# Router scores and squares of a hybrid decoder layer, made for two output blocks at a time in four column groups

## The reference, cut to what matters

```python
x = x + mix                                   # mix = m @ w_out
h = rmsnorm(x, ffn_norm_w)                    # x * rsqrt(mean(x*x) + 1e-6) * w
logits = h @ w_router + b_router              # 1024 -> 32 scores for each token
top_v, top_i = lax.top_k(logits, 4)
gate = softmax(top_v)
x = x + moe(h, top_i, gate)                   # 32 experts, gate_up 1024x2048, down 1024x1024
```

## Time and profile before

| what | value |
|---|---|
| median of 3 runs | 1414.34 us (1414.23 to 1415.02) |
| profiled execution, its own time | 1416.62 us |
| its span, first to last instruction | 1414.3 us |
| mean granted clock of TensorE | 0.995 |
| TensorE busy | 1376.6 us, 97% |
| VectorE, ScalarE, GpSimd busy | 36%, 18%, 8% |
| DMA over the span | 340 GB/s mean, about 430 GB/s in the experts |

### The profile page before, as it was taken

How to read it: one execution, slowest core, us unless ns; L and a number is a source line. 1 busy time by engine, 2 the same in 40 slices (tenths; PEclk the granted TensorE clock), 3 DMA queues, 4 the chain that set the end, 5 groups by cost and what they waited for, 6 DMA issues and landing times.

```text
span 1414.3 us, 17959 instructions
## 1 busy us (share of the span) xinstructions
PE 1376.6 (97%) x7571; PEld 669.2 (47%) x7571; DVE 511.7 (36%) x1090; ACT 255.6 (18%) x467; POOL 108.6 (8%) x107
## 2 busy tenths in 40 slices
PE   8999999999999999999999999999999999999996
PEld 6888885578887533333333333333323333333332
DVE  5655344313112219322432342223422234223423
ACT  3443341122200221111101110111111011011102
POOL 0102110100000001000100010001000011000100
PEclk9999999999999999999999999999999999999999
DMA  7532527554639799999999999999999999999995
GB/s 232 209 129 85 180 76 236 188 176 145 228 120 373 300 413 428 427 428 431 432 428 427 429 432 430 430 427 430 430 429 430 427 430 434 424 428 427 427 427 228
DMA packets 81807, 481.16 MB, mean 340 GB/s; under 512 B 13919, under 2 KB 34831, under 8 KB 61587
## 3 DMA queue, kind: packets, MB, share of 16 engines
q1 hardware_dynamic: 80644, 478.58, 83.1%
q10 hardware_dynamic: 986, 1.08, 0.3%
q0 software_dynamic: 96, 0.33, 0.1%
HBM read 468.85 MB, written 11.26 MB: 339 GB/s over the span
## 4 chain that ended last, share of the span: by engine, by line
PE 81%; DMA 16%; DVE 2%; issue 0%; ACT 0%; DVEq 0%; ACTq 0%
PE bank L1280 25%; PE bank L1304 12%; DMA ring<-in_w_gate_up 11%; PE bank L724 7%; PE bank L712 6%; DMA ring<-in_w_down 5%; PE bank L1252 5%; PE bank L1123 4%; PE bank L993 4%; PE bank L1334 3%; PE bank L1146 2%; DVE Ssg L2204 1%; PE bank L697 1%; PE bank L1260 1%; PE bank L1289 1%; PE bank L1344 1%
## 5 line engine op out<-in xcount | busy, mean ns | idle before, releaser
L1280 PE MATMUL bank<-ring,xT 128*64 128x512 f32 x2048 | 475.5, 602 | 12.1 <-DMA ring<-in_w_gate_up 11.1
L1280 PEld LDWEIGHTS bank<-ring,xT 128*64 128x64 f32 x2048 | 135.7, 137 | 282.5 <-issue 259.0
L2418 DVE TENSOR_TENSOR glu<-bank,bgb 128x512 f32<-128x512 f32 x32 | 22.1, 691 | 569.5 <-PE bank L1280 555.2
L1304 PE MATMUL bank<-ring,acT 128*64 128x512 f32 x992 | 218.7, 592 | 0.9 <-DMA ring<-in_w_down 0.8
L1304 PEld LDWEIGHTS bank<-ring,acT 128*64 128x64 f32 x992 | 71.1, 137 | 142.1 <-issue 140.8
L724 PE MATMUL bank<-HT,wslot 128*128 128x264 f32 x512 | 119.5, 389 | 0.0
L1918 POOL PARTITION_BROADCAST bgb<-hrow x31 | 40.8, 1317 | 979.5 <-DVE lin L2419 768.3
L724 PEld LDWEIGHTS bank<-HT,wslot 128*128 128x128 f32 x512 | 95.3, 190 | 19.7 <-issue 4.6
L712 PE MATMUL bank<-HT,wslot 128*128 128x264 f32 x384 | 89.5, 394 | 0.8 <-DVE HT L1965 0.8
L1252 PE MATMUL bank<-hrow,O 128*64 128x512 f32 x372 | 89.6, 599 | 0.0
L712 PEld LDWEIGHTS bank<-HT,wslot 128*128 128x128 f32 x384 | 73.9, 194 | 15.3 <-issue 2.3
(11 more groups left out here) (429 smaller groups left out, 1167.2 us busy)
## 6 DMA issues: line engine op xcount, KB each, us to landing
ring<-in_w_gate_up SPq DMA_DIRECT2D x44, 4096.0 KB, 26.7
ring<-in_w_down SPq DMA_DIRECT2D x62, 2048.0 KB, 25.3
ring<-in_w_gate_up SPq DMA_DIRECT2D x36, 2048.0 KB, 28.4
wslot<-in_w_in SPq DMA_DIRECT2D x17, 2048.0 KB, 8.2
ring<-in_w_gate_up SPq DMA_DIRECT2D x8, 1024.0 KB, 8.9
out<-Ssg SPq DMA_DIRECT2D x8, 512.0 KB, 5.3
Ssr<-in_state_ret SPq DMA_DIRECT2D x4, 1024.0 KB, 10.3
out<-Ssr SPq DMA_DIRECT2D x4, 1024.0 KB, 8.5
```

Of the source, the lines that this page charges most:

```text
L1280: t = pe.matmul(B[part][64 * g:64 * g + 64, :], block_of(xT, k), w[:, D * part + 512 * g:D * part + 512 * g + 512], start=(k == 0), stop=( ...
L1304: t = pe.matmul(home[64 * g:64 * g + 64, :], block_of(acts, 2 * k + a), w[:, D * a + 512 * g:D * a + 512 * g + 512], start=(k == 0 and a = ...
```

## The change

Scores and squares of two blocks are taken together, each in its own group of 32 columns, so that the two halves of each sum lie apart (scores in partitions 0 to 31 and 32 to 63, squares in 64 to 95 and 96 to 127). `scores(n)` stands in blocks 2, 4 and 6 and once after the blocks. The copy `lgc` has 128 partitions. The turn to tokens becomes two matmuls for each tile of tokens instead of one transpose: lgc's lower half by a constant whose column j is 1 in every row that is j modulo 32 (`C_D4`), which adds the two halves of the scores into bank 1, and its upper half by one column of that constant, which adds the squares into a column of bank 2.

```diff
-        lgc = at("lgc", ct0, [64, TOK])
+        lgc = at("lgc", ct0, [P, TOK])
@@ out_block
-                    if m and k == 4:
-                        score(m - 1)
+                    if m % 2 == 0 and m and k == 4:
+                        scores(m // 2 - 1)
@@
-            def score(m):
-                if m == 0:
-                    pe.wait_ge(s_wr, 32)
-                pe.wait_ge(s_xw, m + 1)
-                pe.matmul(B[2][0:32, 0:TOK], wr[:, m, :], XwT[:, m, :], start=(m == 0), stop=(m == KT - 1))
-                pe.wait_ge(s_sqt, m + 1)
-                pe.matmul(B[2][32:64, 0:TOK], K[:, C_ONE:C_ONE + 32], sqt[:, m % 2, :], start=(m == 0),
-                          stop=(m == KT - 1)).then_inc(s_lg, 1)
+            def scores(n):
+                if n == 0:
+                    pe.wait_ge(s_wr, 32)
+                pe.wait_ge(s_xw, 2 * n + 2)
+                pe.wait_ge(s_sqt, 2 * n + 2)
+                for g in range(4):
+                    m = 2 * n + g % 2
+                    lhsT, rhs = (wr[:, m, :], XwT[:, m, :]) if g < 2 else (K[:, C_ONE:C_ONE + 32], sqt[:, m % 2, :])
+                    t = pe.matmul(B[2][32 * g:32 * g + 32, 0:TOK], lhsT, rhs, start=(n == 0), stop=(n == KT // 2 - 1))
+                t.then_inc(s_lg, 1)
@@ after the blocks
-            score(KT - 1)
+            scores(KT // 2 - 1)
             normed_rows(4)
             pe.wait_ge(s_lgc, 1)
             pe.wait_ge(s_ob, 8)
             for c, r in TILES:
-                t = pe.transpose(B[1][0:r, 64 * c:64 * c + 64], lgc[:, P * c:P * c + r], K[0:64, C_ID:C_ID + 64])
+                pe.matmul(B[1][0:r, 64 * c:64 * c + NE], lgc[0:64, P * c:P * c + r], K[0:64, C_D4:C_D4 + NE],
+                          start=True, stop=True)
+                t = pe.matmul(B[2][0:r, c:c + 1], lgc[64:P, P * c:P * c + r], K[64:P, C_D4:C_D4 + 1], start=True, stop=True)
             t.then_inc(s_lt, 1)
@@ ScalarE
-                after(act, s_lg, 1, m - 1)
+                after(act, s_lg, 1, m // 2)
                 nc.scalar.activation(sqt[:, m % 2, :], XT[:, m, :], ACT.Square).then_inc(s_sqt, 1)
-            act.wait_ge(s_lg, KT)
-            nc.scalar.copy(lgc[:, :], B[2][0:64, 0:TOK]).then_inc(s_lgc, 1)
+            act.wait_ge(s_lg, KT // 2)
+            nc.scalar.copy(lgc[:, :], B[2][:, 0:TOK]).then_inc(s_lgc, 1)
@@
-                sums = B[1][0:r, 0:192].rearrange("p (c n) -> p c n", c=3)[:, first:last, 32:33]
-                nc.scalar.activation(rs[0:r, first:last].unsqueeze(2), sums, ACT.Sqrt, bias=eps[0:r, :], scale=1.0 / D
+                nc.scalar.activation(rs[0:r, first:last], B[2][0:r, first:last], ACT.Sqrt, bias=eps[0:r, :], scale=1.0 / D
```

## The result

The changed kernel takes 1410.84 us (median of 18 runs, 1408.88 to 1412.43) against 1413.85 us of the kernel before beside it (18 runs, 1411.25 to 1415.02): a ratio of 0.9981, with a 95% interval of 0.9975 to 0.9987, or 2.7 us by the ratio. The forecast was 1411.7 us, a gain of 2.7 us. The two medians themselves lie 3.0 us apart.

The account below looks back on a forecast made before the run. The prediction took TensorE's chain to the first expert as the bound, DMA stream following. Blocks 3.03, last visit −0.02 and turn −0.35 gave 2.66 us: 1414.34 − 2.7 = 1411.7 us, range 1409.7 to 1412.9.

Parts of the forecast that it names:

- The bound: Up to the first expert, TensorE's chain sets the time; shifts there reach the end one to one, DMA stream included.
- A visit and its groups: Breaking off output blocks for scores and squares: 0.77 us with two groups, 0.78 with four; blocks gain 3.03 us.
- the slot longer by 0.07 us: Alternative for four-group visits in the blocks: each slot 0.07 us longer, 0.4 us in all over three visits.
- a visit in pairs: Rival in the output blocks: four groups run two by two, 1.26 us a visit, total gain 0.75 us; chance 0.05.
- the change of shape: Within a score in the output blocks: about 0.28 us lost changing from 128 columns to 32 and back.
- New waits: In the output blocks: no visit waits for squares; block 4's weights land with 2.4 us to spare, costing nothing.
- The last visit: After the last block: all four passes start with the squares; loss 0.02 us, at most 0.07.
- The turn: Turn to tokens: six matmuls take 0.74 us against 0.39 for three transposes, a loss of 0.35 us.
- The sum: Whole path to the first expert: 3.03 − 0.02 − 0.35 = 2.66 us gained.
- The clock: Around the gather, 480.9 to 487.8 us: the low clock costs up to 3.4 us and may become cheaper or dearer.
- one sign of being wrong from my own list: Around the gather: forecast wrong if the stretch at 0.5 of the clock changes in length or place.
- a cheaper clock: Rival around the gather: low clock falls elsewhere or not at all, up to 3.4 us more won; chance 0.20.

Follow-up runs that it names:

- before_warm: Kernel before with three more float32 matmuls, outputs unused, in the waits between turn and gather: 1413.97 us, ratio 1.000.
- pairs: Kernel before with two blocks scored per visit, one after the other in the two old column groups, turn unchanged: 1412.33 us, ratio 0.9983.
- second comparison: The changed kernel, unaltered, measured once more beside the kernel before: 1409.96 us against 1413.93, ratio 0.9972.
- turn_alone: Kernel before with only the turn changed, six matmuls in place of three transposes: 1414.07 us, ratio 1.0002.
- late: Changed kernel with blocks 0 to 5 scored in one visit in block 7, eight buffers for squares: 1410.93 us, ratio 0.9983 to the kernel before.

## Why the prediction was right, and where it was off

**The bound.** It was to be the chain over TensorE to the first expert, with the DMA stream moving along. The profiles show it. The path from the first block to the gather was made anything from 36.23 to 41.75 us long, and from the gather to the end it stayed at 931.8 to 932.5 us in eight profiles, at 933.0 in that of `before_warm`, and at 935.1 only in the one with the low clock (932.1 without its 3.07 us). Behind the first expert the chain does go over loads of the ring (DMA has 16% of it on both pages), but these are sent as TensorE releases a block, and so they moved along. TensorE's waits for weights in the experts went from 11.1 us to 13.1 us in the first profile of the changed kernel and to 10.6 in the second, without changing that. But its reason, that the DMA engines stand empty then, held only in part: they ran full to 481.3 us, past the start of the first expert.

**A visit and its groups.** Forecast 0.77 us before and 0.78 us after; measured 0.77 and 0.79. Four groups ran in the slots of two, 0.22 us each, so the slot longer by 0.07 us that the prediction estimated as an alternative did not come; a visit in pairs, for which 1.26 us were forecast, cost 1.22 in `pairs`. The blocks lost 3.01 us, forecast 3.03 (its 5.37 is seven times the unrounded 0.767). The split within a visit was off by little: 0.28 us was put down to the change of shape and is 0.34.

**New waits.** None came. Between visits 32 passes run in 7.32 us, 0.2 us over 32 × 0.2227, and with the 0.58 us booked to the visit that is its 0.78 again; block 4 did not wait for its weights.

**The last visit.** Forecast +0.02 us and at most 0.07; measured +0.09 in the chain. All four matmuls now wait for ScalarE's squares of block 7 ("0.20 <-ACT sqt" in the row of 470.14 us), where the first pair waited for VectorE's scaled rows. So the visit starts 1.05 us after the blocks where it was 0.91, and gets 0.05 back by being shorter. It is the step furthest off in proportion, by 0.07 us.

**The turn.** Forecast 0.74 us, a loss of 0.35; measured 0.74 us in the chain, where the old one was 0.34: a loss of 0.40, and the turn alone shows the same 0.40. The missing 0.05 us is one of reading: the forecast set the new turn against 0.39 us, from the first start to the last end in the timeline, and the chain counts 0.34 for it. The row groups paired, and the tile of 8 tokens did begin 0.20 us after the pass before it instead of 0.11.

**The sum.** 3.01 − 0.09 − 0.40 − 0.04 = 2.48 us on the path against 2.66; the interval of the measured 2.7 us (1.8 to 3.5 us) holds both. That 2.7 comes so near to 2.66 is luck: the second comparison gave 4.0 us. The level, 1410.84 us for 1411.7, was met less well; 0.5 of the 0.9 us is that the kernel before lay at 1413.85 and not at 1414.34. The gain is below the 2.8 us that I had put as what can be told from no change, but the interval of its ratio leaves 1 out.

**The clock.** Here one sign of being wrong from my own list came: the stretch at 0.5 of the clock is not in the profile of the changed kernel. So the first expert came at 480.90 us and not at 482.8; and the DMA engines ahead of it were not at 13 GB/s but at 407. I gave a cheaper clock 0.20, and the profile looks like that rival; but all nine later profiles are without the stretch too, two of kernels with all seven visits in the blocks among them. So its absence doesn't tell what the change did. What the runs show is that it cost 3.07 us in one profile of the kernel before, and that 11 of 74 timed runs of that kernel lay at 1416 us and more. No run of the changed kernel in 26 went over 1412.5 us, but two of the 12 of `turn_alone` did reach 1417.5 and 1419.1 us (clocks of 0.993 and 0.995), and one of the 12 of `late` 1415.4 (0.995), 4.5 us over its median. So the case may be rarer or cheaper after the change; that stays open. It doesn't carry the 2.7 us of the first comparison, where no run of the kernel before lay over 1415.02.

## What to carry to other kernels

Where a small matmul of another shape is wedged into a dense stream, count the visits before the work in them: here a visit cost 0.34 us and a set of two or four column groups 0.45 us. Fill the groups, put sets in a row, and look for a place on the path where the engine waits anyhow; a dearer turn at the end (0.40 us) is paid once. And when a change is worth less than the scatter of the launch, compare lengths of stages within one profile, from a common start, and check with the medians only that they don't disagree.

## What the hardware showed that I had not expected

The start of the output blocks differed by up to 3.05 us (436.14 to 439.19 us) between executions of the same instructions, and all of it was made in the first 20.2 us, most by the first 16 passes of L712, which took 3.80 us in four profiles and 5.34 to 6.33 in the six others: up to 11 of these passes ran at 0.44 us and not 0.22. And one stretch of 6.8 us at a granted clock of 0.5 cost 3.07 us of path in one profile and was in none of the nine others at that place.
